# Conv channel tile 1: 31 depthwise taps from VectorE to diagonal matmuls on TensorE

## What is computed

```python
u = a_val * sigmoid(a_glu)                       # 2048 x 512
u = depthwise_conv(u, conv_w, width=31, pad=15) + conv_b
u = silu(layernorm(u)); y_a = (u @ w_pw + b_pw) * silu(a_gate)
# B: q, k with rotary; w = softmax(s1) - lam * softmax(s2); o = w @ v
y_b = rmsnorm(o, head_g) * (1 - lam_init) * silu(b_gate)
out = rmsnorm(x + concat(y_a, y_b) @ w_out)
```

## Time and profile before

| | |
|---|---|
| median of 2 runs | 712.86 us (710.65 to 715.07) |
| the profiled execution | 711.55 us |
| its span (slowest core, core 5) | 710.5 us |
| spans of the eight cores | 704.8 to 710.5 us |
| mean granted clock of core 5 | 0.934 |
| PE busy | 566.0 us, 80% |
| DVE busy | 524.5 us, 74% |
| ACT busy | 384.8 us, 54% |
| POOL busy | 224.0 us, 32% |

### The profile page before, as it was taken

The page is one execution under the profiler, slowest core; times in us unless marked ns, Lnnn a source line. Parts: engine busy times, 40 slices in busy tenths (PEclk is TensorE's granted clock), DMA queues, the critical chain, the costliest instruction groups (busy, mean ns, idle before and its releaser), DMA issues.

```text
span 710.5 us, 12191 instructions; the slowest of 8 cores (704.8 to 710.5 us)
## 1 busy us (share of the span) xinstructions
PE 566.0 (80%) x4550; PEld 305.0 (43%) x4550; DVE 524.5 (74%) x503; ACT 384.8 (54%) x554; POOL 224.0 (32%) x138
## 2 busy tenths in 40 slices
PE   1135999994798999984989898888989993659995
PEld 1123444441333444453655555555556661413442
DVE  3267129998768999999999999999981125574666
ACT  4053211230222233383989888888889984832443
POOL 7000000002786610021555555555553312410000
PEclk9999999996889999997999999999998998679998
DMA  8895130303003000000000000000000000752785
GB/s 169 173 238 160 83 55 5 59 9 52 1 0 61 1 0 1 0 2 1 2 1 2 1 2 2 1 2 2 2 2 2 2 2 0 170 97 90 241 290 209
DMA packets 19803, 38.96 MB, mean 55 GB/s; under 512 B 2061, under 2 KB 12194, under 8 KB 19490
## 3 DMA queue, kind: packets, MB, share of 16 engines
q1 hardware_dynamic: 8514, 28.13, 12.1%
q0 software_dynamic: 10928, 9.96, 9.8%
q10 hardware_dynamic: 304, 0.10, 0.1%
HBM read 39.76 MB, written 8.39 MB: 68 GB/s over the span
## 4 chain that ended last, share of the span: by engine, by line
DVE 38%; PE 25%; issue 18%; ACT 8%; DMA 7%; POOL 2%; DVEq 1%; ACTq 0%; SPq 0%; POOLq 0%
DVE cT L353 27%; PE PA L394 12%; PE PA L801 6%; DMA xs<-x 5%; ACT Eb L634 5%; DVE at_o L612 2%; PE PB L754 2%; DVE small L606 2%; PE PB L546 2%; POOL QT L429 2%; DMA rows_c<-norm_g 1%; DVE at_o L607 1%; PE PA L588 1%; DMA out<-rbuf 1%; DVE ln_x L730 1%
## 5 line engine op out<-in xcount | busy, mean ns | idle before, releaser
L353 DVE SCALAR_TENSOR_TENSOR cT<-uT,cwh,cT 128x2048 f32<-128x2048 bf16 x120 | 304.6, 2538 | 8.1 <-DVE cT L349 0.5
L634 ACT ACTIVATE Eb<-PA 128x1024 bf16<-128x1024 f32 x256 | 238.9, 1070 | 17.9 <-PE PA L588 17.5
L546 PE MATMUL PB<-Vg,Eb 128*128 128x129 bf16 x2048 | 169.3, 229 | 9.4 <-DVE at_o L612 9.1
L394 PE MATMUL PA<-hT,wsl 128*128 128x512 bf16 x640 | 152.8, 396 | 2.7 <-DVE uT L458 1.9
L546 PEld LDWEIGHTS PB<-Vg,Eb 128*128 128x128 bf16 x2048 | 123.4, 101 | 67.3 <-issue 67.2
L588 PE MATMUL PA<-QT,KT 64*128 64x256 bf16 x1024 | 104.9, 281 | 28.0 <-ACT Eb L634 26.1
L394 PEld LDWEIGHTS PA<-hT,wsl 128*128 128x128 bf16 x640 | 64.5, 101 | 84.7 <-issue 16.4
L618 POOL TENSOR_TENSOR at_t<-at_o 128x512 f32<-128x512 f32 x16 | 40.3, 2519 | 89.5 <-DVE at_o L612 89.5
L588 PEld LDWEIGHTS PA<-QT,KT 64*128 64x128 bf16 x1024 | 34.8, 94 | 58.5 <-issue 35.6
L801 PE MATMUL PA<-wout,hT 128*128 128x512 bf16 x256 | 56.1, 379 | 1.0 <-DVE rbuf L805 0.8
L488 ACT ACTIVATE qbb<-PA 128x512 bf16<-128x512 f32 x32 | 19.1, 598 | 68.9 <-PE PA L394 68.9
(11 more groups left out here) (83 smaller groups left out, 467.5 us busy)
## 6 DMA issues: line engine op xcount, KB each, us to landing
xs<-x SPq DMA_DIRECT2D x32, 512.0 KB, 7.7
out<-rbuf SPq DMA_DIRECT2D x16, 512.0 KB, 4.3
wsl<-w_in POOLq DMA_DIRECT2D x5, 1024.0 KB, 8.9
wsl<-w_in POOLq DMA_DIRECT2D x4, 512.0 KB, 32.0
wout<-w_out POOLq DMA_DIRECT2D x1, 2048.0 KB, 24.8
cosT<-c_cos SPq DMA_DIRECT2D x1, 1024.0 KB, 5.0
sinT<-c_sin SPq DMA_DIRECT2D x1, 1024.0 KB, 7.1
wpw<-w_pw POOLq DMA_DIRECT2D x1, 512.0 KB, 59.0
```

The lines of the kernel that those rows point to most:

```text
L353: ins = nc.vector.scalar_tensor_tensor(out=cTl[ct][:], in0=src, scalar=cwh[:, ct, j:j + 1], in1=cTl[ct][:], op0=ALU.mult, op1=ALU.add)
L394: ins = nc.tensor.matmul(PA[:, a, :], lhsT=wsl[:, slot, dt, ct * 128:(ct + 1) * 128], rhs=hT[:, dt, tc * 512:(tc + 1) * 512], start=(dt == ...
L546: ins = nc.tensor.matmul(PB[:, 2 * st_ + q2, j * 256:j * 256 + 129], lhsT=Eb[:, eb, j, kp * 256 + q2 * 128:kp * 256 + (q2 + 1) * 128], rhs ...
L634: t_e = act.done(nc.scalar.activation(out=Eb[:, eb, :, :], in_=PA[:, 2 * (g % 2):2 * (g % 2) + 2, :], func=AF.Exp, scale=0.125))
```

## The change

The 31 taps of tile 1 leave VectorE's early queue. In their place stand 62 units (2 halves of the tokens times 31 taps). A unit is one VectorE instruction that makes the diagonal matrix `dg` from the identity and a column of `cwh` (bf16, four slots, in the place of `lam4`), and two matmuls of 512 columns that accumulate into `PB` banks 2 and 3. After the 31st unit of a half ScalarE adds the bias and writes `cT1`. Two units are emitted behind each group from slab 2 on. The remaining early taps are spread anew, and `nzc` is made by another operation.

```diff
-    lam4, _ = sb("lam4", [128, 4, 64], F32)
+    lam4, lam4_at = sb("lam4", [128, 4, 64], F32)
+    dg, _ = sb("dg", [128, 4, 128], BF16, at=lam4_at)
-    conv_q = {"early": [(0, j) for j in range(KW)] + [(1, j) for j in range(KW)],
+    conv_q = {"early": [(0, j) for j in range(KW)],
+    pec = {"units": [], "i": 0, "dg_rd": [None] * 4, "ps_rd": [None, None], "n": 0}
+
+    def pe_conv_plan(ct):
+        for cp in range(2):
+            for j in range(KW):
+                pec["units"].append((ct, cp, j))
+
+    def pe_conv_emit(n):
+        for _ in range(n):
+            if pec["i"] >= len(pec["units"]):
+                return
+            ct, cp, j = pec["units"][pec["i"]]
+            pec["i"] += 1
+            slot_ = pec["n"] % 4
+            pec["n"] += 1
+            dve.wait(pec["dg_rd"][slot_], tok_cwh, tok_lam)
+            t_dg = dve.done(nc.vector.tensor_scalar(out=dg[:, slot_, :], in0=identb[:], scalar1=cwh[:, ct, j:j + 1],
+                                                    scalar2=None, op0=ALU.mult))
+            fw = [t_dg]
+            if j == 0:
+                fw += [tok_uT[ct], tok_upad, p1["last"], pec["ps_rd"][0], pec["ps_rd"][1]]
+            pe.wait(fw)
+            ins = None
+            for c_ in range(2):
+                ch = 2 * cp + c_
+                ins = nc.tensor.matmul(PB[:, 2 + c_, :], lhsT=dg[:, slot_, :],
+                                       rhs=uT[:, ct, PADL - 15 + j + ch * 512:PADL - 15 + j + ch * 512 + 512],
+                                       start=(j == 0), stop=(j == KW - 1), skip_group_check=True)
+            t_mm = pe.done(ins)
+            pec["dg_rd"][slot_] = t_mm
+            if j == KW - 1:
+                gate = [p1["xnb_rd"][0], p1["xnb_rd"][1], p1["last"], st["th_rd"][0], st["th_rd"][1]] if ct == 1 else conv_gate["w"]
+                for c_ in range(2):
+                    ch = 2 * cp + c_
+                    act.wait(t_mm, gate, tok_colv)
+                    t_ev = act.done(nc.scalar.activation(out=cTl[ct][:, ch * 512:(ch + 1) * 512], in_=PB[:, 2 + c_, :],
+                                                         func=AF.Identity, bias=colv[:, CB + ct:CB + ct + 1]))
+                    pec["ps_rd"][c_] = t_ev
+                if cp == 1:
+                    conv_prev[ct] = t_ev
+                    for c4 in range(4):
+                        cb_queue.append((ct, c4))
-    EARLY_TAPS = {1: 12, 2: 14, 3: 4, 4: 4, 5: 14, 6: 14}
+    EARLY_TAPS = {1: 8, 2: 8, 3: 3, 4: 3, 5: 5, 6: 4}
...
                 emit_conv("early", 1)
+            if si >= 2:
+                pe_conv_emit(2)
...
         slab_done[si] = last_pe
+        if si == 1:
+            pe_conv_plan(1)
...
+    pe_conv_emit(1000)
     tok_p2_pe = slab_done[6]
...
-        t_nz = dve.done(nc.vector.tensor_scalar(out=nzc, in0=zr[:, :, 1], scalar1=neglam, scalar2=None, op0=ALU.mult))
+        t_nz = dve.done(nc.vector.tensor_tensor(out=nzc, in0=zr[:, :, 1], in1=neglam.to_broadcast([128, 2]),
+                                                op=ALU.mult))
```

## The result

The kernel after takes 795.84 us (median of 11 runs) beside 711.77 us for the kernel before (10 runs): ratio 1.1188, 95% interval 1.1154 to 1.1223. It is 84 us slower; 790 was forecast. The ratio is that of the fast runs: in two runs of each kernel the cores of a die had a lower granted clock and the time was 724 to 847 us. The profiled execution took 795.44 us, its span is 793.8 us (core 4), the other cores lie between 781.9 and 793.3 us.

A forecast was written before the change was run, and what follows sets the result against it. VectorE's depthwise tap led the chain of waits (27% of the span); VectorE bound attention, and with TensorE slab 2. Profiled 711.55 + 90.4 (G's later end) - 12.5 (attention) = 789.5, forecast 790 us, range 733 to 812.

The forecast's parts named there:

- Slab 2: Slab 2: TensorE stalls 3.9 us for the first diagonal, half clock costs 2, the pass change 1; ends at 172.6.
- Q: Q projection with rotary work: diagonals wait for rt1 and GpSimd's add, clock drops; period 8.4 us, stage 128.8 us.
- The price of a diagonal alone: VectorE, one diagonal without waiting: 0.2 to 0.7 us, 0.2 taken; the far end would add 15 us.
- K, V, G: Projections after Q: K 34.5 us, 3.2 less; V and G stay at 55.4; G ends at 391.3, 90.4 later.
- Attention: Attention: round 1 drained 21 us after G's end instead of 33.5, gaining 12.5; then 17.39 us per two rounds.
- The `nzc` edit: Attention drain, L606: could save 7 us over twelve waits, but the new operation waits too; taken as 0.
- The rest: The tail after attention: taken as unchanged.
- A: Rival on Q: the wait is there but the clock stays up; period 6.3 us, time 759; chance 0.17.
- B: Rival on Q: diagonals don't wait for GpSimd, only the round trip remains; period 4.65 us, time 736; chance 0.15.
- C: Rival on Q: added matmuls fill idle TensorE time if diagonals are issued ahead of L490; time 703; chance 0.10.
- The prediction's worst case: Q: GpSimd adds stop both diagonals of a group; period 9.9 us or more, time 811 upwards; chance 0.08.

The follow-up runs named there:

- prebuilt: The changed kernel, but all 31 diagonals are made once ahead of slab 0 and kept in Gt's place for both halves; 704.60 us, ratio 0.9856 to the kernel before.
- the first experiment: The changed kernel, but in Q GpSimd's add of a group is emitted behind the next group's two diagonals and waits for them; 745.42 us.
- the shared version: The changed kernel with diagonals built ahead, only taps 0 to 14 of tile 1 on TensorE, early taps spread anew; 691.58 us, ratio 0.9687 to the kernel before.

## Why the prediction was right, point by point

*Slab 2.* The stall behind the two taps of slab 1 was 4.29 us (3.9 in the prediction):

```profile
132.63 1.87 PE L415 MATMUL PB<-uT,dg 128*128 128x512 bf16 x4 [4.29 <-DVE dg L406]
```

With the 1.62 us between the passes instead of 1, and a mean clock of 0.93 instead of two lost microseconds, the slab is 50.4 us, not 48.4. It also began at 126.4, not 124.2; 1.5 of these 2.2 us are this core's later start of slab 0.

*Q.* The step on which the forecast stood. First conv matmul 186.99 - 183.11 = 3.88 us behind the group at full clock (3.75), 196.14 - 192.06 = 4.08 at half (3.95); period 8.57 (8.4); Q 129.5 (128.8). The agreement is partly luck, since two misses within it offset each other: the mean period was 0.17 us longer than the 8.4 chosen, and each of the two taps cost 1.8 us instead of 2.35, because the tap takes over the wait for the add. The 0.2 us by which the diagonals were put ahead of the add's recorded end was explained by the add's start-up; no run shows that. The rows show a pair that needs 0.41 us ending 0.09 behind the add, so its own work began at least 0.3 us ahead of the add's recorded end. The cause itself was tested from both sides: the block (diagonals of 0.25 us once the add is moved), and the clock (0.98 once TensorE is kept busy, period 6.47). The price of a diagonal alone, 0.2 by choice between 0.2 and 0.7, is 0.16 from start to start (0.41 for two, 0.25 for one).

*K, V, G.* K 33.4 us (34.5): with the units gone it starts without the stall allowed for it. V and G 55.4, as before, taps hidden. G's end 395.1 instead of 391.3: 2.2 from slab 2's start, 2.0 from slab 2, 0.7 from Q, less 1.1 from K, sum 3.8.

*Attention.* Drain of round 1 at G's end + 21.9 (21); gain in all 13.1 us (12.5). The way there differs a little: at the drain of round 1 the gain is 11.6 us and not 12.5, the period of 17.33 instead of 17.39 us per two rounds adds 0.6, and 1.0 comes at once between the drains of rounds 24 and 25, where the late taps end; that step was neither forecast nor explained. The `nzc` edit was rightly put at nothing, and for the right reason.

*The rest*, taken as unchanged, was 2.2 us longer. 788.5 (the sum less the 1 us outside the span) + 3.8 - 0.6 + 2.2 = 793.9, the span of 793.8.

*The rivals.* A's and B's conditions were both false in the kernel after, and both could be made true in it: 771 and 745 us measured, 759 and 736 in the prediction. At G's end (368.4 and 345.0) they lie 8.5 and 8.2 us above these rivals' own sums, 391.3 - 31.4 and 391.3 - 54.5. Of that, 6.0 us lie ahead of Q, which these sums start at 170.6 and the runs at 176.6 (2 of it are the half clock in slab 2, which they took out and the experiments left in), and 3.7 and 3.6 in Q (103.1 against 99.4, and 79.9 against 76.3): A's period was 6.47, and B's two groups with a tap took 3.2 us more than allowed for. K gives back 1.2 and 1.5. The rest of the misses lies behind the last drain (131.0 and 128.7 instead of 125.9). C's 703 was reached with prebuilt diagonals (704.60), and the point at which it was said to decide, the diagonal's place ahead of `rt1`, was borne out for most of Q by the experiment with that order, though not for its time.

## What to carry to other kernels

Before an operation is moved onto the engine that feeds all others, ask who makes its operands and when: a stationary operand made just in time by a queue that itself waits for the group puts a round trip into that engine's stream, and here cost 86 us of Q against 13 us of matmuls. Operands that depend on weights alone can be built once, ahead of the loop. Then move only as much as the other engine is late: 15 of the 31 taps (with the early taps spread anew) gained 3.1%, all 31 gained 1.4%.

## What was not expected

*The clock comes back in every second period.* The prediction had one length for all. Short stretches of Q in the columns of the earlier trace rows, a busy stretch and the idle one behind it, twice:

```profile
187.10:192.40 5.30, 5.30 (x13) 1.61 (x11) 0.00 (x0) 0.04 (x1) 0.00 (x0) 0.50 0.00 0
192.40:196.10 3.70, 0.25 (x1) 0.00 (x0) 3.27 (x4) 0.56 (x1) 2.35 (x1) 0.96 0.00 0
196.10:200.40 4.30, 4.26 (x13) 1.59 (x13) 0.00 (x0) 0.00 (x0) 0.00 (x0) 0.63 0.00 0
200.40:204.10 3.70, 0.25 (x2) 0.00 (x0) 3.27 (x4) 0.60 (x1) 2.35 (x1) 0.81 0.00 0
```

In one period the group runs through at half clock (3.62 us for eight matmuls) and full speed is granted only once TensorE is idle; in the next it is granted within the group (2.64 us). Periods of 9.15 (186.99 to 196.14) and 8.00 us (196.14 to 204.14) follow each other, so that most of the granted full clock falls where there is nothing to do. The mean of the two, 8.6, happens to lie by the 8.4 assumed.

*Only the first of two diagonals pays.* The pair takes 2.07 us from the start of the first to the end of the second, the first alone up to 2.04. Behind a tap that has waited, neither pays. The prediction's worst case, both stopped, never came.

*Full clock with an idle time in every period.* With 1.7 us idle in each period of 4.67 the granted clock was 1.00 (181 to 204 in the first experiment), with 3.5 in each 8.57 the mean was 0.71. A single idle time of 2.45 us, behind a tap in the run with the diagonals issued first, was enough for half clock: the next four conv matmuls took 1.86 instead of 1.03 us.

*The part behind the last drain differs between kernels* whose code there is the same: 125.9 us before, 128.1 after, 133.1 with the diagonals issued first, 126.9 in the shared version, each on its slowest core. It differs as much between the cores of one execution: 123.9 to 126.7 before, 124.4 to 128.2 after, 124.5 to 132.7 prebuilt, 125.3 to 133.1 with the diagonals issued first. The slowest core is picked by just this. So the spread is not shown to come from the edits, its cause is open, and the time of a single execution can't be trusted below about 7 us here.
